# A two-layer streaming encoder step: new order tables, weighing moved to ScalarE, and history rows loaded turned

## The reference

```python
for layer in range(2):
    xp = rms_norm(hp, g[0]); xs = rms_norm(hs, g[0])
    if layer == 0:   # spatial-gating MLP beside attention, one input and one output projection
        mp, ... = ab_mixer_prompt(xp, ...); ms, ... = ab_mixer_sample(xs, ...)
    else:            # pooling mixer: trailing means over windows of 2/4/8/16 frames
        mp, ... = pool_mixer(xp, zeros, ...)
        ms, ... = pool_mixer(xs, state_c_pool[0], ...)   # state: 15 earlier rows of 1024 values
    hp = hp + rms_norm(mp, g[1]); hs = hs + rms_norm(ms, g[1])
    hp = hp + rms_norm(swiglu(rms_norm(hp, g[2]), w_in, w_out), g[3])   # the same for hs
```

## Time and profile before

| | us |
|---|---|
| median of three runs (969.17 to 970.77) | 969.24 |
| profiled execution | 969.97 |
| its span | 968.2 |
| PE busy | 944.1 (98%) |
| DVE busy | 740.8 (77%) |
| ACT busy | 559.8 (58%) |
| chain that ended last: share of PE | 86% |

### The profile page before, as it was taken

The page is one execution under the profiler, slowest core; times in us unless marked ns, Lnnn a source line. Parts: engine busy times, 40 slices in busy tenths (PEclk is TensorE's granted clock), DMA queues, the critical chain, the costliest instruction groups (busy, mean ns, idle before and its releaser), DMA issues.

```text
span 968.2 us, 17823 instructions
## 1 busy us (share of the span) xinstructions
PE 944.1 (98%) x7032; PEld 908.1 (94%) x7032; DVE 740.8 (77%) x1113; ACT 559.8 (58%) x1065; POOL 48.0 (5%) x57
## 2 busy tenths in 40 slices
PE   7999999899999999999999999999999999999997
PEld 6799889899999999999999988989999999999886
DVE  5487554878799999877679888998999887755643
ACT  5642655667555555456567667885555555654552
POOL 0071220000000000000000001100000000000000
PEclk9999999999999999999999999999999999999999
DMA  8324113465645444447655585454444443666553
GB/s 271 89 69 119 44 45 87 120 175 167 175 129 144 137 132 133 124 120 210 182 160 162 154 221 158 136 148 120 133 140 132 131 136 97 184 171 189 197 173 113
DMA packets 246611, 138.66 MB, mean 143 GB/s; under 512 B 15226, under 2 KB 237794, under 8 KB 246528
## 3 DMA queue, kind: packets, MB, share of 16 engines
q1 hardware_dynamic: 246064, 137.06, 49.2%
q0 software_dynamic: 224, 0.35, 0.1%
q10 hardware_dynamic: 240, 0.10, 0.0%
HBM read 134.91 MB, written 2.58 MB: 142 GB/s over the span
## 4 chain that ended last, share of the span: by engine, by line
PE 86%; DVE 7%; issue 3%; ACT 2%; DMA 1%; POOL 1%; ACTq 0%; DVEq 0%; POOLq 0%
PE ps L810 14%; PE ps L812 13%; PE ps L811 13%; PE ps L1290 12%; PE ps L1292 12%; PE ps L1291 12%; DVE wlo L2045 2%; PE ps L1240 2%; PE ps L1242 2%; PE ps L1241 2%; DMA raw<-in_ffn_w_in_dram 1%; PE ps L1179 1%; ACT whi L1437 1%; DVE xa L2326 1%; POOL rs L2838 1%
## 5 line engine op out<-in xcount | busy, mean ns | idle before, releaser
L2045 DVE TENSOR_TENSOR wlo<-raw,whi 128x1024 fp32r<-128x1024 f32 (+3 forms) x232 | 230.4, 997 | 81.6 <-ACT whi L1437 81.1
L1437 ACT ACTIVATE whi<-raw 128x1024 fp32r<-128x1024 f32 (+3 forms) x232 | 199.3, 864 | 72.9 <-PE ps L812 52.9
L1290 PE MATMUL ps<-xhi,whi 128*128 128x288 f32 (+1 forms) x528 | 154.3, 292 | 1.0 <-ACT tmp L1946 1.0
L1292 PE MATMUL ps<-xhi,wlo 128*128 128x288 f32 (+1 forms) x528 | 153.8, 291 | 0.0
L1291 PE MATMUL ps<-xlo,whi 128*128 128x288 f32 (+1 forms) x528 | 153.1, 290 | 0.0
L811 PE MATMUL ps<-mlo,whi 128*128 128x288 f32 (+1 forms) x528 | 152.9, 290 | 0.0
L2045 DVE TENSOR_TENSOR wlo<-t,whi 128x1024 fp32r<-128x1024 f32 x86 | 105.1, 1222 | 29.4 <-ACT whi L1437 29.4
L810 PE MATMUL ps<-mhi,whi 128*128 128x288 f32 (+1 forms) x368 | 108.1, 294 | 0.0
L812 PE MATMUL ps<-mhi,wlo 128*128 128x288 f32 (+1 forms) x368 | 107.7, 293 | 0.0
L1240 PE MATMUL ps<-xhi,whi 128*128 128x256 f32 x352 | 102.8, 292 | 4.8 <-ACT p L1900 3.3
L1290 PE MATMUL ps<-shi,whi 128*128 128x288 f32 x352 | 104.6, 297 | 1.9 <-DVE slo L2521 0.9
(11 more groups left out here) (300 smaller groups left out, 2118.5 us busy)
## 6 DMA issues: line engine op xcount, KB each, us to landing
raw<-in_ffn_w_in_dram SPq DMA_DIRECT2D x177, 256.0 KB, 3.4
raw<-in_ffn_w_in_dram SPq DMA_DIRECT2D x44, 512.0 KB, 4.1
raw<-in_ffn_w_out_dram SPq DMA_DIRECT2D x48, 384.0 KB, 3.8
raw<-in_ffn_w_out_dram SPq DMA_DIRECT2D x48, 320.0 KB, 3.5
raw<-in_ffn_w_out_dram SPq DMA_DIRECT2D x22, 512.0 KB, 3.9
raw<-in_ab_w_in_dram SPq DMA_DIRECT2D x10, 512.0 KB, 5.3
raw<-in_ab_w_out_dram SPq DMA_DIRECT2D x10, 256.0 KB, 3.0
raw<-in_ab_w_out_dram SPq DMA_DIRECT2D x20, 128.0 KB, 3.3
```

The source lines that it names most:

```text
L1290: pe.matmul(out, wh, hi[:, k, :], start=opens and k == 0, stop=False, skip_group_check=True)
L1292: mm = pe.matmul(out, wl, hi[:, k, :], start=False, stop=k == KC // 2 - 1, skip_group_check=True)
L1437: act.activation(whi[:, m % NSPLIT, 0:n], split_source(m), ACT.Copy).then_inc(w_hi, 1)
L2045: dve.tensor_tensor(wlo[:, s, 0:n], split_source(m), whi[:, s, 0:n].bitcast(F32), ALU.subtract)\
```

## The change

It has five parts. (1) The state rows are fetched value by value, turned, straight into `xf`, during the attention; `turn_hist`, `hist_high` and the tile `hist` are gone. (2) In the first seam and in the first chain ScalarE multiplies h by the gain (`weigh_first`, `weigh`), and VectorE multiplies by r_pre only; the load of the Silu table moves. (3) The last unit's second half product moves from the end of `fast_first` into `fast_rest`, behind a term, and the first two terms swap. (4) ScalarE and VectorE split and copy in another order around that place. (5) New tables: `FIRST` for the chain of layer 0, other slots in `CHAIN`.

```diff
 CHAIN = {
-    "PE": {"sum": 1, "spread": 1, "hist": 3.5, "pre": 4, "again": 4.5, "c": (5, 5, 5.5, 5.5), "rows": (6, 6), "sum2": 10.5,
+    "PE": {"sum": 0.5, "spread": 0.5, "pre": 3.5, "again": 4, "c": (5, 5.5, 5.5, 5.5), "rows": (5.5, 5.5),
...
@@ block.sync, before the loads of the output projection
+            turned = state[0, 0].rearrange("t (k p) -> p k t", p=P)
+            for k in range(KC):
+                sp.dma_start(xf[:, k, TOK:TOK + HIST], turned[:, k, :], allow_slow_non_contiguous=True).then_inc(hist_loaded, 16)
+                sp.dma_start(xf[:, k, TOK + HIST:TOK + HIST + 1], turned[:, k, HIST - 1:HIST], allow_slow_non_contiguous=True).then_inc(hist_loaded, 16)
@@ at the load of ("p", 1, 4)
-                    sp.dma_start(hist[0:HIST, :], state[0, 0]).then_inc(hist_loaded, 16)
-                    sp.dma_start(hist[HIST:HIST + 1, :], state[0, 0, HIST - 1:HIST, :]).then_inc(hist_loaded, 16)
@@ block.tensor
-            def turn_hist():
-
-                pe.wait_ge(hist_loaded, 64)
-                for k in range(KC):
-                    mm = pe.transpose(flat(4, k * DEC, HIST + 1), hist[:, k * P:(k + 1) * P], ident[0:HIST + 1, 0:HIST + 1])
-                mm.then_inc(hist_turned, 1)
@@ plain_pool_products
-                    pe.wait_ge(hist_hi, 1)
+                    pe.wait_ge(hist_loaded, 16 * (2 * KC + 2))
@@ fast_first, end, and fast_rest
-                second(FC - 1)
                 run(LAST)
+                return second
...
                 for f in range(FC):
...
+                    early = f == 0
                     pe.wait_ge(w_lo, split_no(ma))
+                    if early:
+                        pe.wait_ge(silu_done, inner(layer, 0, FC - 4) + 1)
+                        pe.wait_ge(x_lo_done[1], 4 * layer + 4)
+                        term(ma, 0, 2 + f % 2, *s1, n, True)
                     pe.wait_ge(p1_seeded, i + 1)
...
                     term(ma, HALF, f % 2, *s2, n, False).then_inc(sum_done, 1)
+                    if f == 0:
+                        second(FC - 1)
@@ block.scalar, after_mixer_ab
+                act.wait_ge(out_stored, 16 * STORES_AB)
+                weigh_first(0)
+                weigh_first(1)
                 hi_part(U_OUT + 11)
                 root(0, 0, 1)
-                warm(ACT.Silu)
                 keep_spread(0, 0, 1)
+                weigh_first(2)
+                weigh_first(3)
+                x_high(0, 0, 0)
+                x_high(0, 0, 1)
                 evacuate_out(12)
-                for p in range(4):
-                    x_high(0, 0, p)
+                hi_part(U_OUT + 12)
+                x_high(0, 0, 2)
+                x_high(0, 0, 3)
@@ fast_rest of block.scalar
+                    if f == 0:
+                        keep_sum(0, 0)
+                        gelu_gate(FC - 1)
+                        hi_part(AT["ta", layer, 1])
+                        keep_sum(0, 1)
+                        seed(layer, 1)
+                        s_high(layer, 3)
@@ block.vector, x_scale
+                if s == 0:
+                    dve.wait_ge(weighed, p + 1)
+                    dve.tensor_tensor(x_pair(0, 0, p), x_pair(0, 0, p), pair_of(r_pre, 0), ALU.mult).then_inc(x_scaled[0], 1)
+                    return
```

## The result

| kernel | median of its runs | profiled execution | span |
|---|---|---|---|
| before, same comparison | 969.78 us (969.17 to 970.77, 4 runs) | 969.97 us | 968.2 us |
| after | 977.83 us (977.40 to 979.36, 4 runs) | 977.60 us | 975.7 us |

The ratio of the times is 1.008, 95% interval 1.0068 to 1.0093: 8 us **slower**, where 963.5 us (range 960.0 to 969.7) was predicted.

What follows compares the result with a forecast made beforehand. TensorE's stream of matmuls was taken as the bound, with gaps in the first and pooling seams. Terms -1.95 - 1.0 - 0.2 - 1.0 - 2.0 - 0.7 + 1.1 = -5.75 us on 969.24 gave 963.5 us, range 960.0 to 969.7.

Steps and rivals of the forecast that it cites:

- The single values: Attention: 16 DMAs fetching 16,384 single history values ahead of the output weights were priced at 0 us.
- slack of 21.6 us: Attention: time the DMA queue had for the single values before the first output unit's split at 101.35 us.
- stated ends of 19.6 and 31 ns: Price per piece, from 256-byte pieces and from the whole run; about 20 and 32 us for the history's loads.
- Rival 3: Attention: single values hold up the output weights; at 31 ns each 10.1 us late, 973.6 us; chance 0.13.
- First seam: After the first output projection: ScalarE weighs xa, gaps for xlo and p close, -1.95 us (0 to -2.6).
- Rest of the first chain: Layer 0's chain: squarings queued behind p close a 1.02 us gap, -1.0 us; p ahead of a split, -0.2 us.
- start of layer 0's second half: Layer 0 product: reordered terms cover the seed, slo and the next split, -1.0 us.
- Layer 1: Start of layer 1's second half: the same reordering removes gaps of 0.47, 0.89 and 0.35 us and restarts, -2.0 us.
- The transposes: Pooling seam: eight history transposes (0.66 us) leave TensorE, -0.7 us (-0.5 to -0.8).
- The pooling table: Pooling seam: TensorE's earlier sum and spread wait 1.5 us longer, 0.4 returned, +1.1 us (0 to +3.2).
- the remaining slots: Other places of splits and pool products shift work between engines that keep up: 0, with 1 us either way.
- rival 2: Pooling seam loses what others gain; a second slow-clock stretch costs 1.7 us; 967.2 or 968.2 us; chance 0.08.

Runs made afterwards that it cites:

- nine loads: Kernel after with the eight small single-value loads (128 values each) made one, same 16,384 values in the same place: 974.73 us, ratio 1.004.
- Four pairs: Kernel after with four of eight pairs of single-value loads in the attention, the other four behind half-units of layer 0's second half: 968.18 us, ratio 0.9974.
- eight pairs: Kernel after with the 16 single-value loads on SyncE's queue, a pair behind every fourth half-unit of layer 0's second half: 968.28 us, ratio 0.998.
- six pairs: Kernel after with six of the eight pairs of single-value loads in the attention, two later: 970.58 us, ratio 0.9997.
- new table and GpSimd's loads: Kernel after with its 16 single-value loads issued by GpSimd's queue behind its last power of layer 0's norm: 984.44 us, ratio 1.0143.
- first sum put back: Kernel after with GpSimd's loads, only TensorE's first pooling sum and spread back from 0.5 to 1: 983.79 us.

## Why the prediction was wrong, step by step

- **The single values** (term 0, measured +10.9). The slack of 21.6 us was nearly right: half the pieces cost nothing, and ScalarE's first wait puts it at about 19.2 us (76.7 to 95.9), since the first unit took 5.9 us and not 3.3 to be ready. The step that failed is "I take under 20 us, since 256 bytes is nearer". The pieces took 28.7 us, 28 ns for each of an engine's 1,024, inside the stated ends of 19.6 and 31 ns. The row nearest by bytes was the wrong neighbour: a packet of 4 bytes was indeed short (9.6 ns), but it was not the packet that set the pace. "SP itself is no danger: 16 issues at 0.4 us are 6.4 us" failed with it; issues stood up to 3.97 us.
- **Rival 3** named the mechanism, the place and the sign, with a chance of 0.13. By its own rate 28.7 - 21.6 = 7.1 us of lateness; ScalarE's wait was 10.04, as the slack was shorter and the first unit was ready only 6.4 us after its queue came free. Of the 10.9 us lost, 8.46 are TensorE's wait; the other 2.4 are what the lower clock took (4.9 us of work at half the clock), which no term had. With nine loads 4.04 us of wait and 10 x (1 - 0.73) = 2.7 us make 6.7 of the 7.0. The page that spoke against the change, the Trainium skill's "DMA: Bandwidth & Descriptors", section "Rules for kernel authors", was borne out: for the 16,384 elements SyncE's queue moved 16,608 packets more over the whole run (246,064 before, 262,672 after). That they held it for 28.7 us is this case's measurement.
- **First seam** (-1.95): right. TensorE's idle time there fell from 2.61 to 0.63 us, and it waits 0.24 us for the first xlo where it was 0.93. The seam alone makes -1.9 between matmuls 800 and 900.
- **Rest of the first chain, start of layer 0's second half** (-1.2, -1.0): between the same matmuls -1.2 (900 to 1,200) and -1.9 (1,200 to 1,480), of which the idle time of the windows 201 to 241 and 241 to 273 shows 1.02 and 1.07 us. The places were right, and the second gave 0.9 us more than its term. The wait of 0.50 us for the second tmp stayed, as foreseen. **Layer 1** (-2.0): -2.4.
- **The transposes** (-0.7): 0.4 us, below the lower end of 0.5; the 0.66 us of their row were not all on the path.
- **The pooling table** (+1.1, with the transposes +0.4; measured +4.7). The first sum's wait grew by 1.44 us as worked out. The step that failed is "the next sum, reached earlier by the chain than by TensorE's stream, gives 0.4 back" and, with it, "the remaining slots: I take 0". The next sum waited 1.96 us more, since ScalarE now squares behind p, and a second stretch at half the clock came: 4.00 x (1 - 0.57) = 1.7 us, the size that rival 2 had. The three make 5.1 us, less the transposes' 0.4 the 4.7 measured.
- **The sum.** -5.75 predicted. The orders brought 0.95 + 0.4 more, the pooling seam 4.3 less, and the attention cost 10.9: -5.75 - 1.35 + 4.3 + 10.9 = +8.1; the medians differ by 8.05.

## What to carry to other kernels

A transfer is priced by its pieces and by how long it holds its queue, not by its bytes; where its price lies between two ends and the slack ends between them, "free" is only one of two forecasts, and the price should be measured before the sum takes it as nothing. Ask of a wait not only how long it is but whether the clock falls with it: here 2.6 us more of lateness cost 5.6. Since the same waits came with and without such a fall, compare two orders by their medians and not by one trace alone. And an order table is a whole: places that are each harmless by their wait did not add up, in either direction.

## What the runs showed of the hardware

- 4-byte pieces on SyncE's queue: it stood 1.75 ns for each in sixteen loads (28.7 us for 16,384) and 1.48 ns in nine (24.3 us), with the 16 engines a third busy. One load of 128 pieces stood up to 3.97 us behind one of 1,920 that stood 0.44 us; where the eight large loads follow each other (nine loads) they stood 21.6 us together.
- On GpSimd's queue the same pieces slowed the weight loads of SyncE's queue: 15.8 us to land instead of 3.9. Four pairs 15.6 us apart on SyncE's queue cost nothing, eight pairs 8 us apart 2.2 us.
- The clock fell to half with waits of TensorE of 4.04 and 8.46 us in the attention (in the second during the wait, between 108 and 112 us), and in the seam after one of 1.56 us; after 0.44 us (six pairs) it stayed at full speed.
- The length of a wait does not settle it: after 0.35 and 1.91 us the clock was 0.72 in 566 to 572 in one kernel and 1.00 in another, and after 1.96 us at the second sum it fell with the new table and GpSimd's loads and stayed at 1.00 with the first sum put back.
